# A two-layer hybrid diffusion backbone: the first feed-forward layer by seven products, with five of its modulation jobs, two more behind the first mixer and one in the last layer

## The reference

```python
def swiglu(t, w_in, w_out):
    gate, up = jnp.split(t @ w_in, 2, axis=-1)
    return (jax.nn.silu(gate) * up) @ w_out
...
h = h + 0.5 * m[:, 2] * swiglu(modulate(h, m[:, 0], m[:, 1]), w_ff1_in[l], w_ff1_out[l])
...
h = h + m[:, 5] * y          # y: the mixer of this layer
h = h + 0.5 * m[:, 8] * swiglu(modulate(h, m[:, 6], m[:, 7]), w_ff2_in[l], w_ff2_out[l])
```

## Time and profile before

| what | value |
| --- | --- |
| median of 3 runs | 3273.53 us (3271.9 to 3273.64) |
| profiled execution, device time | 3272.6 us |
| its span, first to last instruction | 3270.8 us |
| PE / DVE / ACT / POOL busy share | 95% / 59% / 34% / 8% |
| mean granted TensorE clock | 0.982 |

### The profile page before, as it was taken

How to read it: one execution, slowest core, us unless ns; L and a number is a source line. 1 busy time by engine, 2 the same in 40 slices (tenths; PEclk the granted TensorE clock), 3 DMA queues, 4 the chain that set the end, 5 groups by cost and what they waited for, 6 DMA issues and landing times.

```text
span 3270.8 us, 43730 instructions
## 1 busy us (share of the span) xinstructions
PE 3102.8 (95%) x17735; PEld 2739.3 (84%) x17735; DVE 1938.7 (59%) x2755; ACT 1110.4 (34%) x1734; POOL 266.0 (8%) x317
## 2 busy tenths in 40 slices
PE   5999999999999998898999999999999998999999
PEld 4999999987669895488999988999998876678887
DVE  7754536524552536757778765877778548643333
ACT  4211212356441321235323334532323436632222
POOL 1100000200001005620000001000000100000000
PEclk8999999999999999999999999999999999999999
DMA  6533424411004220012343321333333120023332
GB/s 209 169 102 108 124 72 137 127 36 52 7 1 129 59 64 14 1 39 70 112 129 104 116 65 59 110 97 102 111 116 110 56 61 8 14 83 97 96 97 90
DMA packets 314304, 274.20 MB, mean 84 GB/s; under 512 B 17426, under 2 KB 290057, under 8 KB 313865
## 3 DMA queue, kind: packets, MB, share of 16 engines
q1 hardware_dynamic: 286992, 182.35, 18.7%
q0 software_dynamic: 25488, 89.14, 8.7%
q10 hardware_dynamic: 1641, 0.14, 0.0%
HBM read 263.21 MB, written 8.39 MB: 83 GB/s over the span
## 4 chain that ended last, share of the span: by engine, by line
PE 50%; DVE 4%; ACT 2%; issue 1%; POOL 0%; ACTq 0%; DVEq 0%
PE ps L2236 28%; PE ps L497 16%; PE ps L1453 1%; DVE hs_lo L2437 1%; ACT gpt L1492 1%; DVE vw_lo L2169 1%; ACT gp L1505 1%; PE ps L1211 1%; PE ps L1477 1%; PE ps L1435 1%; PE ps L2318 0%; DVE ms_s L2468 0%; DVE h_sb L2445 0%; PE ps L1891 0%; PE ps L1908 0%
## 5 line engine op out<-in xcount | busy, mean ns | idle before, releaser
L487 DVE TENSOR_TENSOR w_lo<-ring,w_hi 128x1024 fp32r<-128x1024 f32 (+3 forms) x221 | 251.4, 1139 | 450.2 <-ACT w_hi L472 361.7
L497 PE MATMUL ps<-u_hi,w_hi 128*128 128x384 f32 (+2 forms) x1584 | 469.1, 356 | 19.6 <-DVE u_lo L663 15.4
L497 PE MATMUL ps<-u_lo,w_hi 128*128 128x384 f32 (+2 forms) x1584 | 461.9, 351 | 0.0
L497 PE MATMUL ps<-u_hi,w_lo 128*128 128x384 f32 (+2 forms) x1584 | 461.5, 351 | 0.0
L472 ACT CAST w_hi<-ring 128x1024 fp32r<-128x1024 f32 (+3 forms) x157 | 149.4, 952 | 612.3 <-PE ps L497 574.1
L497 PEld LDWEIGHTS ps<-u_hi,w_hi 128*128 128x128 f32 x1584 | 284.9, 190 | 47.9 <-issue 23.2
L497 PEld LDWEIGHTS ps<-u_lo,w_hi 128*128 128x128 f32 x1584 | 286.4, 190 | 22.7 <-issue 1.7
L2169 DVE TENSOR_TENSOR vw_lo<-ring,vw_hi 128x1024 fp32r<-128x1024 f32 (+1 forms) x176 | 211.2, 1200 | 155.6 <-ACT vw_hi L2163 155.3
L497 PEld LDWEIGHTS ps<-u_hi,w_lo 128*128 128x128 f32 x1584 | 285.4, 189 | 21.2
L2163 ACT CAST vw_hi<-ring 128x1024 fp32r<-128x1024 f32 (+1 forms) x176 | 181.3, 1030 | 330.5 <-PE ps L2236 267.4
L2236 PE MATMUL ps<-u_hi,vw_hi 128*128 128x384 f32 x768 | 249.0, 338 | 11.8 <-DVE u_lo L663 10.9
(11 more groups left out here) (350 smaller groups left out, 5854.8 us busy)
## 6 DMA issues: line engine op xcount, KB each, us to landing
ring<-in_w_ff_in SPq DMA_DIRECT2D x176, 512.0 KB, 4.0
ring<-in_w_ff_out SPq DMA_DIRECT2D x72, 512.0 KB, 4.0
cst<-in_w_mod POOLq DMA_DIRECT2D x72, 512.0 KB, 3.9
m_in<-in_w_mod POOLq DMA_DIRECT2D x56, 512.0 KB, 4.0
ring<-in_w_in_e SPq DMA_DIRECT2D x26, 512.0 KB, 3.9
m_first<-in_w_mod POOLq DMA_DIRECT2D x16, 512.0 KB, 13.9
ring<-in_w_out_e SPq DMA_DIRECT2D x16, 512.0 KB, 3.8
ring<-in_w_ff_out SPq DMA_DIRECT2D x16, 384.0 KB, 3.4
```

The lines of the kernel that those rows point to most:

```text
L487: dve.tensor_tensor(w_lo[:, b:b + WIDE[n]], ring[:, s:s + WIDE[n]], w_hi[:, b:b + WIDE[n]], ALU.subtract).then_inc(w_split_lo, 1)
L497: mm = pe.matmul(ps_at(p, c0, c1) if halved else pair(p)[:, c0:c1], w, x[:, c0:c1], start=start and i == 0, stop=stop and i == 2)
```

## The change

Block 0 too is run by seven products. Its planner gets a table of its own: 17 DVE entries (job (0, 2), 16 items and the fold) lie on P and A1, with 3, 3, 2, 1 items on P's chunks and 1, 1, 1, 2, 2, fold on A1's chunks 0 to 5; later bodies take 2, 2, 1, 1 on the chunks o = 2, 3, 4, 6. Block 0 has five jobs. Jobs (2, 1) and (2, 0) move into `dve_mla_out`, four or five entries after each residual, with new buffers `ms_m` and `m_in_m` in memory that the attention has left; PE makes their matmuls after output chunk 4 and ahead of projection chunk 2. `pool_fetch` now alternates a piece of `w_mod` with each fetch of the saved input, and each piece waits until the piece two before it has been used. Block 2 keeps four jobs; (5, 2) moves to part 0 of block 3, with its fold and matmuls in that part's output product. In all blocks the D step comes one chunk earlier, on the chunk of the PE step. Nothing of the computation is left out.

```diff
-STR = (1, 2)
+STR = (0, 1, 2)
...
+        ms_m, m_in_m = at("ms_m", 32 * T, 2 * D), at("m_in_m", 32 * T + 2 * D, 2 * D)
...
-        MODS = {(0, 0): [(0, 2), (1, 1), (1, 0)], (0, 1): [(1, 2), (2, 2)], (0, 2): [(2, 1), (2, 0)],
+        MODS = {(0, 0): [(0, 2), (1, 1), (1, 0)], (0, 1): [(1, 2), (2, 2)], (MLA, 0): [(2, 1), (2, 0)],
                 (1, 0): [(3, 1), (3, 0)], (1, 1): [(3, 2)], (1, 2): [(4, 2)],
-                (2, 0): [(4, 1), (4, 0)], (2, 1): [(5, 2)], (2, 2): [(5, 1), (5, 0)]}
+                (2, 0): [(4, 1), (4, 0)], (2, 1): [(5, 1), (5, 0)], (3, 0): [(5, 2)]}
-        MODS_AT = {1: (0, 2)}
-        SEAM_BANKS = {1: (4, 5)}
+        MODS_AT = {}
+        SEAM_BANKS = {}
...
                 for e, x in enumerate((u_hi, u_lo)):
+                    n = MLA_FIRST + 2 * d + e
+                    pool.wait_ge(m_used, n - 1)
+                    pool.dma_start(in_rotary(n), mod_src(MLA_JOBS[d // 4], n % DB)).then_inc(m_full[n % 2], 16)
                     pool.dma_start(x[:, d, :], kept[e, d]).then_inc(u_back, 16)
...
+                if r == R_MLA and d == 4:
+                    pe_s_mod(pe, MLA_JOBS[0], ms_m)
...
+                if q == 2:
+                    pe_s_mod(pe, MLA_JOBS[1], ms_m)
+                if q == 3:
+                    pe.wait_ge(mod_raw, JOB[MLA_JOBS[1]] + 1)
...
+                if i == 1:
+                    dve_s_mod_item(dve, ("d", MLA_JOBS[1]), ms_m, in_rotary)
...
+            urgent = {("P", 0, 0): 3, ("P", 0, 1): 3, ("P", 0, 2): 2, ("P", 0, 3): 1, ("A", 1, 0): 1, ("A", 1, 1): 1,
+                      ("A", 1, 2): 1, ("A", 1, 3): 2, ("A", 1, 4): 2, ("A", 1, 5): 1} if i_f == 0 else {}
+            usual = {2: 2, 3: 2, 4: 1, 6: 1} if i_f == 0 else {2: 1, 3: 2, 4: 1}
             for c, ch in enumerate(S_ORDER[i_f]):
-                cap = {2: 1, 3: 2, 4: 1}.get(ch[2], 0) if ch[0] == "A" else 3
-                if ch[0] == "P":
-                    cap = 0
+                cap = 3 if ch[0] == "O" else usual.get(ch[2], 0) if ch[0] == "A" else 0
+                if urgent and ch[0] != "O" and ch[1] < 2:
+                    cap = urgent.get(ch, 0)
...
+        MLA_TODO = [x for q, job in enumerate(MLA_JOBS)
+                    for x in [("p", job, k, MLA_FIRST + DB * q + k, s) for k in range(DB) for s in range(2)] + [("f", job)]]
...
                 dve_residual(dve, R_MLA, d)
+                if d == 5:
+                    dve_s_mod_item(dve, ("d", MLA_JOBS[0]), ms_m, in_rotary)
+                for x in MLA_TODO[17 * d // 4:17 * (d + 1) // 4]:
+                    dve_s_mod_item(dve, x, ms_m, in_rotary)
...
-            pe_ff(pe, 0)
+            pe_s_ff(pe, 0)
             pe_norm(pe, 1)
+            pe.wait_ge(const_back, 16)
...
+            pool_mod(pool, 3, 0)
```

More of the change, by code:

```diff
@@ L392, in build @@
         RES = {r: DB * i for i, r in enumerate(RUN)}
-        MODS = {(0, 0): [(0, 2), (1, 1), (1, 0)], (0, 1): [(1, 2), (2, 2)], (0, 2): [(2, 1), (2, 0)],
+        MLA = 0.5
+        MODS = {(0, 0): [(0, 2), (1, 1), (1, 0)], (0, 1): [(1, 2), (2, 2)], (MLA, 0): [(2, 1), (2, 0)],
                 (1, 0): [(3, 1), (3, 0)], (1, 1): [(3, 2)], (1, 2): [(4, 2)],
-                (2, 0): [(4, 1), (4, 0)], (2, 1): [(5, 2)], (2, 2): [(5, 1), (5, 0)]}
+                (2, 0): [(4, 1), (4, 0)], (2, 1): [(5, 1), (5, 0)], (3, 0): [(5, 2)]}
         NORM_BY = {R_FF(0, LAST(0)): 1, R_SSD: 2, R_FF(1, LAST(1)): 3, R_FF(2, LAST(2)): 4, R_GQA: 5}
-        MODS_AT = {1: (0, 2)}
-        SEAM_BANKS = {1: (4, 5)}
+        MODS_AT = {}
+        SEAM_BANKS = {}
         JOBS = [(0, 1), (0, 0)] + [x for key in sorted(MODS) for x in MODS[key]]
@@ L2097, in build @@
                     plan[c]["pe"].append(done)
-                if busy >= 0 and c == busy + 3:
                     plan[c]["dve"].append(("d", done))
@@ L2124, in s_wait_buffer @@
             else:
-                back_to_back = i_f - 1 in STR and i_f > 1
+                back_to_back = i_f == 2 and 1 in STR
                 if back_to_back:
@@ L2310, in pe_s_out_chunk, with pe_s_mod @@
                 mm.then_inc(o_mm, 1)
-        def pe_s_mod(pe, x):
+        def pe_s_mod(pe, x, m):
             pe.wait_ge(m_fold, HALVED.index(x) + 1)
@@ L2317, in pe_s_mod @@
                 c0 = 16 * x[1] + 2 * d
-                pe.matmul(bank(6, c0, c0 + 1), ms_s[0:64, P * d:P * d + P], ones[0:64, 0:1], start=True, stop=True)
-                mm = pe.matmul(bank(7, c0, c0 + 1), ms_s[64:128, D + P * d:D + P * d + P], ones[64:128, 0:1],
+                pe.matmul(bank(6, c0, c0 + 1), m[0:64, P * d:P * d + P], ones[0:64, 0:1], start=True, stop=True)
+                mm = pe.matmul(bank(7, c0, c0 + 1), m[64:128, D + P * d:D + P * d + P], ones[64:128, 0:1],
                                start=True, stop=True)
@@ L2325, in pe_s_ff @@
                 for x in S_MODS[i_f][c]["pe"]:
-                    pe_s_mod(pe, x)
+                    pe_s_mod(pe, x, ms_s)
                 if ch[0] == "P":
@@ L2448, in dve_s_residual, with in_constants, in_rotary, dve_s_mod_item @@
             x.then_inc(o_res, 1)
-        def dve_s_mod_item(dve, i_f, x):
+        def in_constants(n):
+            return cst[:, C_BLK + D * (n % 2):C_BLK + D * (n % 2) + D]
+        def in_rotary(n):
+            return m_in_m[:, D * (n % 2):D * (n % 2) + D]
+        def dve_s_mod_item(dve, x, m, w_at):
             if x[0] == "d":
@@ L2454, in dve_s_mod_item @@
                 dve.wait_ge(m_used, n_first + DB * (JOB[x[1]] - 1))
-                dve.tensor_tensor(ms_s[0:64, 0:D], ms_s[0:64, 0:D], ms_s[64:128, 0:D], ALU.add)
-                dve.tensor_tensor(ms_s[64:128, D:2 * D], ms_s[0:64, D:2 * D], ms_s[64:128, D:2 * D], ALU.add).then_inc(m_fold, 1)
+                dve.tensor_tensor(m[0:64, 0:D], m[0:64, 0:D], m[64:128, 0:D], ALU.add)
+                dve.tensor_tensor(m[64:128, D:2 * D], m[0:64, D:2 * D], m[64:128, D:2 * D], ALU.add).then_inc(m_fold, 1)
             else:
                 _, job, k, n, s = x
-                w = cst[:, C_BLK + D * (n % 2):C_BLK + D * (n % 2) + D]
-                at_, by = ms_s[:, D * s:D * s + D], sc[:, 2 * k + s:2 * k + s + 1]
+                w = w_at(n)
+                at_, by = m[:, D * s:D * s + D], sc[:, 2 * k + s:2 * k + s + 1]
                 if s == 0:
@@ L2582, in dve_s_ff @@
                         dve_s_prod(dve, i_f, 0, 1, 1)
+                    for x in items:
+                        dve_s_mod_item(dve, x, ms_s, in_constants)
                     continue
@@ L2634, in dve_s_ff @@
                 for x in items:
-                    dve_s_mod_item(dve, i_f, x)
+                    dve_s_mod_item(dve, x, ms_s, in_constants)
         def sync_ff(f, i_f):
@@ L2660, in act_mla_out @@
                 act_split(act, b + d + 2)
+        MLA_JOBS = MODS[MLA, 0]
+        MLA_FIRST = n_first + DB * (JOB[MLA_JOBS[0]] - 2)
+        MLA_TODO = [x for q, job in enumerate(MLA_JOBS)
+                    for x in [("p", job, k, MLA_FIRST + DB * q + k, s) for k in range(DB) for s in range(2)] + [("f", job)]]
         def dve_mla_out(dve):
@@ L2682, in _ @@
                 sp.dma_start(xin[:, n, :], src).then_inc(x_in, 16)
-            sync_ff(f, 0)
+            sync_s(f, 0)
             assert f.n == BASE["even"]
@@ L2745, in _ @@
             pe_norm(pe, 4)
-            pe.wait_ge(const_back, 16)
+            pe.wait_ge(const_back, 32)
             pe_items(pe, n_even, len(items), 4)
@@ L2809, in _ @@
             for c in range(2):
-                act_split(act, BASE[NEXT[0]] + c)
+                act_s_split(act, 0, c)
             for d in range(DB):
                 act_shift(act, 0, 0, d)
-            act_ff(act, 0)
+            act_s_ff(act, 0)
             act_norm(act, 1)
@@ L2854, in _ @@
             for c in range(2):
-                dve_split(dve, BASE[NEXT[0]] + c)
+                dve_s_split(dve, 0, c)
             dve_mod(dve, JOBS[1], 1, (5, 2))
             dve_norm(dve, 0)
-            dve_ff(dve, 0)
+            dve_s_ff(dve, 0)
             dve_norm(dve, 1)
+            dve.wait_ge(const_back, 16)
             dve_items(dve, 0, n_even)
@@ L2876, in _ @@
             dve_norm(dve, 4)
-            dve.wait_ge(const_back, 16)
+            dve.wait_ge(const_back, 32)
             dve_items(dve, n_even, len(items))
@@ L2889, in _ @@
             pool_mod_first(pool)
-            for part in PARTS:
-                pool_mod(pool, 0, part)
+            pool_s_mod(pool, 0)
             pool_squares(pool, 1)
@@ L2894, in _ @@
             pool_fetch(pool)
+            pool.wait_ge(const_back, 16)
             for g in range(2):
```

4 lines of the change are left out of this document (2 added, 2 removed).

## The result

The change made the kernel slower: 3296.68 us median (3293.7 to 3299.52, four runs) against 3272.72 (3267.62 to 3273.64, four runs) for the kernel before in the same comparison, a ratio of 1.0073 with a 95% interval of 1.0061 to 1.0085. Forecast were 3263 and a range of 3254 to 3276. The profiled execution's span is 3294.5 us, 23.7 more than before; PE is idle 208.9 us of it (3294.5 - 3085.6), 40.9 more than before. It is busy 17.2 us less than in the earlier trace rows, though the 240 matmuls that are gone had been priced at 41.6. Much of the difference is TensorE's clock: the mean granted clock is 0.976 in place of 0.982, and 0.024 x 3294.5 less 0.018 x 3270.8 is 20 us. That is an estimate and an upper bound, as part of it falls into idle time.

The account below looks back on a forecast made before the run. PE, 95% busy, was taken as the bound. Block 0 -17.3, first mixer +14, block 2 -9 and block 3 +2.1 sum to -10.2 us, giving a 3263 us median; the 8-in-10 range was 3254 to 3276.

Parts of the forecast that it names:

- I start from block 1's 546.05 and cost what differs: Block 0: block 1's window as base, plus 10 and 2 us, giving 558, 17.3 us less than before.
- P and A1: Block 0's first bodies, holding the first job's 17 entries: DVE late by 10.3 us, taken as 10, bounds 4 to 16.
- the fifth job's PE step: Block 0: its 1.88 us fall into the wait at the first output part, so nothing was added.
- Items hidden in the later bodies: Block 0: two more items per body stay under 29.26 us; only chunk 6's before output parts cost 2 us.
- Rival 2: DVE bounds part of block 0: half of 19 extra items exposed, 12 us, 3275, no measurable change; chance 0.27.
- Rival 3: DVE bounds all of block 0: all 19 extra items exposed, 24 us, 3287, slower; chance 0.10.
- The mixer: First mixer with two jobs: fold wait 2.9, two PE steps of 1.88, fetch 5.3, low clock 2; 14 us more.
- fetch: First mixer: PE waits 5.3 us (4.4 to 8.9) before the projection for the last fetch of the saved input.
- is done before PE, held by the fetch, gets there: First mixer: projection chunk 1's split, delayed by the second job's last items, costs PE nothing.
- its folds move by a chunk or two, under cover of PE: Block 1: the shifted folds cost nothing, so its time stays unchanged.
- Block 2: Without its fifth job it becomes as long as block 1: 9 us less, between 6 and 11.
- Block 3: One job in part 0's output product: PE waits 0.2 and works 1.88, 2.1 us more, between 1.9 and 5.

Follow-up runs that it names:

- x1_seam: The changed kernel with the second and third buffers of split weights exchanged in block 0; 3292.44 us, ratio 1.0049 to the kernel before.
- x4_thin: The changed kernel with block 0's items behind each job's first two cut to 16 columns, leaving out the five jobs' sums; 3281.31 us, ratio 1.0020.
- x7_plan0: The changed kernel with four items per later body in block 0 and no fold on an output part's first three chunks; 3288.69 us, ratio 1.0049.
- x2_plan: The changed kernel with the D step one chunk later again in blocks 1 and 2; 3286.34 us, ratio 1.0040 to the kernel before.
- x8_part3: The kernel before the change, with only job (5, 2) moved from block 2 to part 0 of block 3; 3269.73 us, ratio 0.9993.
- x6_mixer: The changed kernel with both mixer jobs laid out anew: four items ahead of the first output chunk, a separate first sum, earlier fetches; 3277.38 us, ratio 1.0012.

## Why the prediction was wrong

The measured time is 34 us above the forecast: block 0 accounts for 12.0 of it, the mixer for 10.7, block 1 for 5.3, block 2 for 3.6, block 3 for 2.2. No one step did it. The plan of the sum held; single waits were left out or mis-sized, and the clock behind them was priced in one place only.

- **Block 0, the start from block 1's time.** This step failed most quietly. "I start from block 1's 546.05 and cost what differs" left out that another stage follows: the norm's seam cost 5.6 us (38.9 + 10.0 in place of 34.1 + 9.2 for the last output part and the norm; x1_seam).
- **P and A1.** Near, by two errors that nearly cancel. The bodies take 77.22 less 68.30, 8.9 us more, for which I had 10.3; the fifth job's PE step, which I took to fall into that wait, came on top with 1.9. I had 10, it is 10.8. Of the 8.9, DVE's items are 6.8 (x4_thin).
- **Items hidden in the later bodies.** Wrong by 3.5: 22.86 of 29.26 us is a sum, and the place of one late piece inside it decides (x7_plan0; A6 and A7 alone are 3.2 of it). The output parts cost 4.0 in place of 2. Together with the above this is all of 569.98 - 546.05 = 23.9. Rival 2 was right in its place, and its 12 us of exposed items were more than the 7.5 seen. Rival 3, which alone had forecast a slower kernel, was wrong in its mechanism: DVE is busy 419 us of block 0's 570.
- **The clock in block 0.** Of the same 23.9 us, 13.9 are idle time and 10.0 are PE busy for longer. The PE step is 1.9 of these. The sum had no term for the rest; the granted clock, 0.98 in place of 0.99, gives 0.02 x 570 less 0.01 x 546, some 6 us, as an estimate.
- **The mixer.** Fold 3.7 for 2.9, steps as forecast, fetch 9.0 for 5.3, its low clock 1.5 for 2. The missing term is the 2.7 us of low clock behind the first wait. The fetch's term was mis-sized twice. I had its issue 1.0 us behind the end of chunk 7 (1064.2 and 1063.2) and the landing 4.3 behind the issue. Measured, PE ended chunk 7 at 1060.5 and the last fetch was issued at 1063.33, 2.8 behind, as DVE's items had stood 1.55 us for a piece; PE started 6.2 later, at 1069.5. The two pieces for which DVE waited landed 6.6 and 5.6 us after their issue. My own sentence that the second chunk's split "is done before PE, held by the fetch, gets there" was right: it ended near 1074.7, the first chunk near 1079.4.
- **The scan behind the projection**, from the projection's last matmul to the first of the next output product, takes 183.3 us for 179.7. 1.3 of it is idle time; the rest is PE busy for longer, at a granted clock of 0.94 in place of 0.96. No wait that the change makes explains it. The stretch takes 178.2 to 183.3 us over all eleven kernels without order, so I count it as variation; its cause stays open.
- **Block 1, "its folds move by a chunk or two, under cover of PE".** Wrong: I looked at the bodies and not at the residual behind the fold. Block 1 is 4.8 us longer than in x2_plan and block 2 is 2.1 longer; 2.5 and 1.9 of that are PE's idle time, the rest its clock.
- **Block 2.** The 9 us were right: 8.6 with the old plan (x8_part3).
- **Block 3.** Wait and PE step come to 2.15 us, for which I had 2.1. The other 2.1 had no term: 1.6 of them is low clock behind the step, as in this window right behind it:

```profile
3018.70:3021.30 2.60, 2.60 (x8) 2.01 (x7) 0.00 (x0) 0.00 (x0) 0.00 (x0) 0.50 0.00 0
```

The Trainium skill ("SBUF — State Buffer", "Who interferes with whom") says that an operation of DVE in a two-port mode blocks GpSimd, and that transfers which GpSimd issues can stall by it; it names copy, cast and tensor_scalar for such modes, while all but the first two items of a job are SCALAR_TENSOR_TENSOR. The runs do not show such an effect: pieces issued in block 0 landed in 4.1 us in the median in the changed kernel, and in 4.8 in x4_thin, where DVE's items were nearly gone (though the pieces were issued closer together).

```profile
cst<-in_w_mod POOLq DMA_DIRECT2D x40, 512.0 KB, 4.1
```
```profile
cst<-in_w_mod POOLq DMA_DIRECT2D x40, 512.0 KB, 4.8
```

That the memory's load made the mixer's last pieces late (218 GB/s in the window against 66 before) is likely, but only argued.

## What to carry to other kernels

When a stage is replaced by one whose time is known from elsewhere, price its seams and every wait that depends on a parity or a slot, not its inside alone. Where a planner is shifted by one step, list which operation stands ahead of each operation that PE waits for, before and after. When a stall is removed, compute the second latest condition first: behind the fetch stood a split that held PE for another 4.2 us, and only a layout that cured both gave the time back. And give each wait of PE, and each of its short steps, a term for the lower clock that may follow: in block 0 that was some 6 us which the sum didn't have.

## What the runs showed of the hardware

Behind the mixer's first PE step (32 one-column matmuls after a wait of 3.4 us) matmuls ran at 1.2 GHz and 2.7 us were lost. Behind the step in block 3, which PE had entered with a wait of under 0.3 us, PE worked for 1.5 us at full pace, then the granted clock was 0.50 for the 2.6 us shown above, and eight matmuls took 0.427 us each in place of 0.23: 1.6 us. In x6_mixer the step without a wait was followed by full clock throughout. In the kernel before, four of the nine steps in blocks 1 and 2 were followed by ten or eleven matmuls at the low pace, though PE waited before none of them: two bodies with such a step take 61.95 us, with another step 60.4. In the changed kernel it is four of the thirteen steps in blocks 0 to 2. What decides stays open; 1.5 us behind one step in three is no small term beside a step's 1.88.
